# The mixer of a two-layer hybrid block: output products of a state-space chunk moved from the end of an even unit to the head of the odd unit behind it, and the next head's q turned ahead of a chunk

## The reference, cut to what matters

```python
def gqa_attend(qblk, k, v):
    s = jnp.einsum('bqgrd,bkgd->bgrqk', qblk, k).astype(jnp.float32) * (HEAD_DIM ** -0.5)
    p = jax.nn.softmax(s, axis=-1).astype(v.dtype)
    return jnp.einsum('bgrqk,bkgd->bqgrd', p, v)
...
    Lmat = jnp.exp(segsum(a))
    scores = jnp.einsum('bclhn,bcshn->bhcls', Cc, Bc) * Lmat
    y_diag = jnp.einsum('bhcls,bcshp->bclhp', scores, x)
    y_off = jnp.einsum('bclhn,bchpn,bhcl->bclhp', Cc, prev_states, jnp.exp(a_cs))
    return (y_diag + y_off).reshape(Bsz, L, H, P), final
```

## Time and profile before

| what | value |
|---|---|
| median of 3 runs | 1579.82 us (1579.38 to 1581.22) |
| the profiled execution, whole | 1580.66 us |
| its span in the profile | 1578.8 us |
| PE busy, share of the span | 1523.1 us, 96% |
| DVE, ACT, POOL busy | 868.0, 595.1, 138.9 us |
| chain that ended last | PE 84%, DVE 7%, ACT 4% |

### The profile page before, as it was taken

One profiled execution on the slowest core, in us unless ns is written; L12 is line 12 of the kernel. 1 busy time (PEld: TensorE's weight loads), 2 busy tenths in 40 slices (PEclk: granted clock), 3 DMA queues, 4 the chain that ended last, 5 costly groups with the idle time before them and its releaser, 6 DMA issues.

```text
span 1578.8 us, 22083 instructions
## 1 busy us (share of the span) xinstructions
PE 1523.1 (96%) x8944; PEld 1374.1 (87%) x8944; DVE 868.0 (55%) x1174; ACT 595.1 (38%) x900; POOL 138.9 (9%) x150
## 2 busy tenths in 40 slices
PE   6999988999999999999999999998999999999998
PEld 4899857899999999999999998995778788888887
DVE  4678887546755545555553467457656333333333
ACT  6634477535422112221122345346646321222222
POOL 0230421020000000000000024023110000000000
PEclk9999999999999999999999999998999999999999
DMA  9556221023443333333431133312022333333322
GB/s 366 169 174 190 68 77 41 19 63 113 141 133 113 127 132 109 134 127 113 133 112 52 51 80 88 79 57 67 15 67 81 94 99 99 91 88 102 93 77 83
DMA packets 208105, 162.49 MB, mean 103 GB/s; under 512 B 9268, under 2 KB 191004, under 8 KB 207900
## 3 DMA queue, kind: packets, MB, share of 16 engines
q1 hardware_dynamic: 206588, 156.63, 32.0%
q10 hardware_dynamic: 1440, 4.78, 0.8%
HBM read 156.76 MB, written 2.15 MB: 101 GB/s over the span
## 4 chain that ended last, share of the span: by engine, by line
PE 84%; DVE 7%; ACT 4%; issue 2%; DMA 1%; SPq 0%; POOL 0%; DVEq 0%; ACTq 0%; POOLq 0%
PE banks L1874 70%; PE banks L1992 4%; PE banks L2143 2%; PE banks L2021 1%; PE banks L2049 1%; DVE mod_sum L1320 1%; DVE w_lo L1295 1%; PE banks L2120 1%; DMA raw<-in_w_in_dram 1%; DVE nrm L1397 1%; PE banks L2176 1%; DVE h_lo L1391 1%; DVE neg_max L1675 1%; PE banks L1826 1%; ACT nrm L932 1%
## 5 line engine op out<-in xcount | busy, mean ns | idle before, releaser
L1295 DVE TENSOR_TENSOR w_lo<-raw,w_hi 128x1056 fp32r<-128x1056 f32 x184 | 245.1, 1332 | 298.3 <-ACT w_hi L879 297.5
L1874 PE MATMUL banks<-h_hi,w_hi 128*128 128x384 f32 (+3 forms) x1296 | 387.2, 357 | 10.2 <-DVE h_lo L1391 4.7
L1874 PE MATMUL banks<-h_lo,w_hi 128*128 128x384 f32 (+3 forms) x1296 | 382.9, 354 | 0.0
L1874 PE MATMUL banks<-h_hi,w_lo 128*128 128x384 f32 (+3 forms) x1296 | 382.6, 353 | 0.0
L879 ACT ACTIVATE w_hi<-raw 128x1056 fp32r<-128x1056 f32 x184 | 198.3, 1078 | 245.1 <-PE banks L1874 227.4
L1874 PEld LDWEIGHTS banks<-h_hi,w_hi 128*128 128x128 f32 x1296 | 235.6, 189 | 40.2 <-DVE h_lo L1391 10.6
L1874 PEld LDWEIGHTS banks<-h_hi,w_lo 128*128 128x128 f32 x1296 | 238.0, 189 | 16.8
L1874 PEld LDWEIGHTS banks<-h_lo,w_hi 128*128 128x128 f32 x1296 | 237.7, 189 | 15.8
L1874 PE MATMUL banks<-g_hi,w_hi 128*128 128x384 f32 (+1 forms) x528 | 159.9, 357 | 0.0
L1874 PE MATMUL banks<-g_hi,w_lo 128*128 128x384 f32 (+1 forms) x528 | 159.3, 356 | 0.0
L1874 PE MATMUL banks<-g_lo,w_hi 128*128 128x384 f32 (+1 forms) x528 | 159.2, 355 | 0.0
(11 more groups left out here) (223 smaller groups left out, 1891.6 us busy)
## 6 DMA issues: line engine op xcount, KB each, us to landing
raw<-in_w_dram SPq DMA_DIRECT2D x120, 512.0 KB, 3.9
mod_ring<-in_w_mod_dram SPq DMA_DIRECT2D x96, 512.0 KB, 4.9
raw<-in_w_in_dram SPq DMA_DIRECT2D x32, 512.0 KB, 4.9
raw<-in_w_out_dram SPq DMA_DIRECT2D x16, 512.0 KB, 4.2
raw<-in_w_dram SPq DMA_DIRECT2D x16, 384.0 KB, 3.3
cb_rows<-cs_rows_dram SPq DMA_DIRECT2D x20, 256.0 KB, 3.4
x_in<-in_x_dram ACTq DMA_DIRECT2D x4, 512.0 KB, 8.2
out_dram<-x_out SPq DMA_DIRECT2D x8, 256.0 KB, 2.3
```

Source lines behind the costliest of these rows:

```text
L1295: dve.tensor_tensor(w_lo[n % 2][:, :], raw[n % 4][:, :], as_f32(w_hi[n % 2][:, :]), ALU.subtract).then_inc(lo_ready, 1)
L1874: ins = pe.matmul(to(p, a, b), ws[:, w], xs(k, a, b), start=(first and q == 0), stop=(last and q == 2))
```

## The change

Three edits, all in the order of the list; no instruction is added or taken out.

1. `ssd_w` of a chunk moves from the head of the even unit to its end, behind the maximum, the copy of `p_T` and whatever `in_unit` places there. `ssd_y` moves from the end of the even unit to the head of the next odd unit.
2. `tr q` moves ahead of the `ssd` of its unit, and ahead of the gate products that share its place. With edit 1 it also comes ahead of `ssd_y` in units 2 and 12 of layer 0 and unit 6 of layer 1.
3. In layer 1, `("q01", 3)` moves ahead of the first turn of k.

```diff
             else:
-                ev += [states[0], blocks[3], states[1], ("q01", 2), ("tr", "k", 0), states[2], ("q01", 3), ("tr", "k", 1), states[3],
+                ev += [states[0], blocks[3], states[1], ("q01", 2), ("q01", 3), ("tr", "k", 0), states[2], ("tr", "k", 1), states[3],
                        ("tr", "q", 0), ("q23_squares",), states[4]]
...
             for u in range(len(units) + 3):
-                if last_c is not None:
-                    ev.append(("ssd_w", last_c, u))
+                if last_c is not None and u % 2:
+                    ev.append(("ssd_y", last_c))
+                    last_c = None
...
                 ev += in_unit.get(u, [])
                 gate_now = not todo and last_c is None
                 if last_c is not None:
-                    ev.append(("ssd_y", last_c))
-                    last_c = None
+                    ev.append(("ssd_w", last_c, u))
                 if gate_now and gates and gates[0][0] in ("gs", "gi"):
                     ev.append(gates.pop(0))
+                if u < len(units) and units[u][1] == (2 if l and units[u][0] == 1 else 1) and units[u][0] + 1 < ATT_HEADS:
+                    ev.append(("tr", "q", units[u][0] + 1))
                 if todo and u % 2:
                     last_c = todo.pop(0)
                     ev.append(("ssd", last_c))
...
-                if u < len(units) and units[u][1] == (2 if l and units[u][0] == 1 else 1) and units[u][0] + 1 < ATT_HEADS:
-                    ev.append(("tr", "q", units[u][0] + 1))
```

## The result

The changed kernel took 1598.87 us (median of 5 runs) against 1580.98 us beside it: ratio 1.0113, 95% interval 1.0101 to 1.0125, 17.9 us slower. The profiled execution has a span of 1597.2 us against 1578.8, 18.4 us more. The forecast was 1586.2 us, 6.4 us slower: the sign was right, the size by far too small, and the measured time lies outside the range.

The account below looks back on a forecast made before the run. PE bounds the kernel, idling only in the mixers. Layer 0 +2.5, layer 1 -0.6 and clock +4.5 give +6.4 us on the median 1579.82: 1586.2 us, range 1579.0 to 1591.0.

Parts of the forecast that it names:

- What bounds the kernel: Mixers: PE idles 8.2 us of 40 in layer 0, 4.2 in layer 1; any PE hold goes into the end.
- Edit 1, the order on DVE: Mixers: w falls behind the maximum, copy and extra work; extra work is added in full to y's wait.
- Edit 2: Mixers: the 3.86 and 2.87 us gaps go; ACT's exponentials start about 1.6 us later in unit 7, layer 0.
- Edit 3: Layer 1, rotation ahead of k's turn: 0.2 us gained, bounds 1.0 lost and 1.9 gained.
- The clock: Two new gaps, 5.5 and 4.1 us, followed by clock 0.50, 2.25 us each: together +4.5 us.
- The sum with the clock held: Mixers at clock 1.00: +2.5 us in layer 0 and -0.6 us in layer 1.
- w beside POOL: Mixers: w running while POOL works on e_cum counted as nothing; bound about 0.7 us on each of 10 chunks.
- the faster one (w_hi early): Unit 8: ACT reaches w_hi 3 us or more earlier, the weight tile doesn't hold w; 1575.8 us, chance 0.16.
- The slower one: w second to POOL, or a lapse behind unit 2's 3.7 us gap in layer 0; +3 to +4, 1590, chance 0.15.
- w late behind the weight tile: Unit 8, both layers: w waits behind w_lo; PE gaps 5.5 us in layer 0, 4.1 in layer 1.

Follow-up runs that it names:

- run 1: The kernel before with only edit 1 (w at the end of the even unit, y heading the odd one): 1602.17 us, ratio 1.014.
- run 4: The changed kernel with w back at the head of the even unit: 1579.76 us, ratio 0.9992.
- run 5: The changed kernel with w ahead of its unit's extra work, still behind the maximum and the copy: 1584.12 us, ratio 1.0021.
- run 6: The changed kernel with only the weight tile of unit 8 moved behind w, in both layers: 1588.32 us, ratio 1.0049.
- edit3_alone: The kernel before with only edit 3, q's rotation in layer 1 ahead of the first turn of k: 1580.25 us, ratio 0.9996.
- after_filled_short: The changed kernel with PE's gaps filled by 5 to 21 products of the identity by itself: 1588.7 us, ratio 1.0042.
- Run 11: The changed kernel with the shorter gap fill and POOL's products on e_cum cut to 4 of 128 columns: 1588.48 us, ratio 1.0052.
- run 8: The same run as after_filled_short, the changed kernel with PE's gaps filled by the shorter fill: 1588.7 us, ratio 1.0042.
- after_pool_small: The changed kernel, gaps unfilled, with POOL's products on e_cum cut to 4 of 128 columns: 1596.31 us, ratio 1.0104.

## Why the prediction was too small

**What bounds the kernel:** right. What PE lost in the mixers went into the end. One reading was off: w keeps y waiting at three later chunks (0.84, 0.65 and 1.33 us), not four.

**Edit 1, the order on DVE:** right in place and mechanism, shown by runs 1 and 4 to 6. The loss by parts, each from one run to the next and so with an error of about 2 to 3 us: edits 2 and 3 without edit 1 at -3.5 us; q's turn ahead of y +2.2; w behind the maximum and the copy +4.6; q's extra work ahead of w +4.4; the weight tile ahead of w +10.1. Each step holds the lapses of the clock that it brings.

**Edit 2:** right that the gaps of 2.87 and 3.86 us go, and that in layer 0 the gain is swallowed in unit 8. Alone it is a gain of 4.1 us.

**Edit 3:** right that it can't be told from nothing.

**The clock:** this is the step that failed. I wrote that two new gaps, 5.5 and 4.1 us, would be followed by 0.50, and held the 3.7 and 2.5 us gaps harmless because 2.91 and 2.87 had been so in the earlier trace rows; the gaps in units 4 and 6 of layer 0 and in unit 4 of layer 1 I did not weigh for a lapse at all. Slow work followed all seven: 3.85, 2.00, 2.79 and 5.60 us in layer 0, 2.62, 1.84 and 4.41 in layer 1. The term was +4.5 us, two lapses of 2.25; filling the gaps took back about 10, seven lapses of 1.3 to 1.6. The count was wrong; the price was not too low.

The trace of the kernel before already spoke against it. Behind the 1.88 us gap at 1068.62 S of unit 0 took 2.08 us instead of 1.12, at a granted clock of 0.50. I did not read that S:

```profile
1070.06 2.08 PE L2120 MATMUL banks<-k_T,q_T 128*128 128x512 f32 x2
```

```profile
1070.00:1072.00 2.00, 2.00 (x5) 0.92 (x4) 1.06 (x2) 1.98 (x2) 0.36 (x1) 0.50 0.00 0
```

Over all sixteen traces, from 206 us on in layer 0 and in the mixer of layer 1: behind each of the 17 gaps of 3.24 us or more a lapse came, before the gap ended or within 1.5 us of its end. Gaps of 1.84 to 2.91 us went either way: after 2.87 the turn of P took 0.84 in the kernel before and 1.51 in edit3_alone. The slow work need not be the first instruction behind the gap. After 3.86 us in edit1_alone the turn of q took the usual 0.84, and the S behind it 2.01:

```profile
211.12 0.84 PE L2021 MATMUL banks<-tab,qk 128*128 128x128 f32 x6 [3.86 <-issue]
...
214.20 2.01 PE L2120 MATMUL banks<-k_T,q_T 128*128 128x512 f32 x2
```

**The sum with the clock held:** +2.5 and -0.6 us counted, 7 to 9 measured. By the starts of S in after_filled_short, counted from S of unit 0, layer 0 is 5.1 us longer than before at unit 13 (2.5 counted), and layer 1 is 2.4 longer at unit 10 (0.4 shorter counted). In layer 0 1.2 of the 2.6 us too few had arisen by S of unit 5, where the trace has y waiting twice for w, the second time 0.60 us in the middle. In layer 1 the three pairs of units 3 to 9 took 11.71, 10.82 and 13.43 us where I had counted 9.85, 9.55 and 12.85: 3.7 too few, hidden in part by 1.8 us won ahead of unit 2, most of it because the lapse on S of unit 0 is gone. The first two of these pairs have the same 0.60 in the middle of y. That is w beside POOL. I had priced it at nothing on the ground that w's twenty records did not vary. They did not because w stood ahead of POOL's product there; moving w changed just that. Run 11 against run 8, less what the same cut gives in the kernel before, puts it at about 1.8 us in these two pairs. The rest of what was counted too little is not pinned to a term.

**The rivals:** the faster one (w_hi early) did not come: w_hi started at 249.35 in layer 0. The slower one named both things that happened, a lapse behind the gap in unit 2 of layer 0 and w second to POOL, but with +3 to +4 us and a chance of 0.15. The sign of the forecast owes nothing to luck, since w late behind the weight tile was right and alone cost 10 us; the size was short in both of its terms.

## What to carry to other kernels

When engines walk a common list in order, an event's price is what stands ahead of it on its own engine: one weight split placed ahead of the product that PE was waiting for cost 10 us over two places, though it had always been in the same unit. In a kernel like this one, price every new gap on PE of about 2 us or more with the work behind it at half clock as well, read two or three instructions past each gap for it, and take gaps that passed without harm in one execution as luck until several show it. A duration that never varied says nothing about a place in which the instruction never stood.

## What the runs showed of the hardware that was not expected

- Gaps of 1.84 to 2.79 us on PE were followed by the 1.2 GHz level in the changed kernel, and gaps of one length (2.87, 2.91) came out either way between executions of kernels that differ elsewhere. What decides was not settled.
- Work for PE in the gap, products of the identity that nobody reads, kept the clock at 1.00 in the filled stretches and was worth about 10 us in the changed kernel. It must be sized from the trace: 46 float32 products of 128 columns showed as 92 instructions in 10.43 us, 0.11 us each.
- w beside POOL took up to 1216 ns in the changed kernel, and up to 1745 beside the larger rotation (after_pool_small), against 693 at most before. The Trainium skill, page "SBUF — State Buffer", section "Who interferes with whom", states that a DVE instruction with two SBUF inputs contends with a GpSimd instruction that reads SBUF, the loser waiting in full. By that rule w in second place waits for POOL's instruction, and the traces agree: w's longest record is 1210 ns or more in all eight kernels in which it stands late, and 694 or less in the eight in which it stands first.
